# Moving the accumulator of a 31-tap depthwise convolution from SBUF to two PSUM banks

## What is computed

```python
h = rmsnorm(x, norm_mix_g)
z = h @ w_in                                   # 1024 -> 3*512 + 2*512
a_h, a_bg, a_cg, b_val, b_gate = split(z)      # 512 channels each
y_a = a_bg * dwconv(a_cg * a_h, conv_a_w)      # 3 taps
u = b_val * sigmoid(b_gate)
u = dwconv(u, conv_b_w) + conv_b_b             # 31 taps, 512 channels: the change
y_b = silu(layernorm(u, ln_b_g, ln_b_b))
x = x + concatenate([y_a, y_b]) @ w_out
```

## Time and profile before

| | |
|---|---|
| median of three runs | 2363.95 us |
| lowest and highest | 2361.16 and 2364.13 us |
| profiled execution, span from first to last instruction | 2362.2 us |
| PE busy | 2139.1 us (91% of the span) |
| DVE busy | 1606.9 us (68%) |
| POOL busy | 1067.2 us (45%) |
| ACT busy | 508.6 us (22%) |
| granted TensorE clock, mean | 0.963 of full |

### The profile page before, as it was taken

One profiled execution on the slowest core, in us unless ns is written; L12 is line 12 of the kernel. 1 busy time (PEld: TensorE's weight loads), 2 busy tenths in 40 slices (PEclk: granted clock), 3 DMA queues, 4 the chain that ended last, 5 costly groups with the idle time before them and its releaser, 6 DMA issues.

```text
span 2362.2 us, 24514 instructions
## 1 busy us (share of the span) xinstructions
PE 2139.1 (91%) x9224; PEld 1711.3 (72%) x9224; DVE 1606.9 (68%) x1645; ACT 508.6 (22%) x992; POOL 1067.2 (45%) x459
## 2 busy tenths in 40 slices
PE   3988868799999999999959999999999879879996
PEld 2876746588888888888737888788777558657885
DVE  8999987856666556667798455464483870795647
ACT  2211112321111111111232101001010331685112
POOL 6544553535544444456264353263262432342722
PEclk8998979999999999999979999999999989999998
DMA  4130111133123222333011111121021021000201
GB/s 145 38 97 27 36 36 36 36 134 101 61 87 107 97 94 93 107 107 107 27 45 41 40 46 53 36 62 44 29 69 36 18 71 30 16 28 1 72 18 72
DMA packets 42952, 141.71 MB, mean 60 GB/s; under 512 B 3568, under 2 KB 7808, under 8 KB 42880
## 3 DMA queue, kind: packets, MB, share of 16 engines
q1 hardware_dynamic: 29984, 101.38, 13.4%
q10 hardware_dynamic: 12896, 39.36, 4.7%
HBM read 136.50 MB, written 7.36 MB: 61 GB/s over the span
## 4 chain that ended last, share of the span: by engine, by line
PE 64%; DVE 31%; issue 2%; ACT 1%; POOL 1%; DMA 0%; DVEq 0%; SPq 0%; ACTq 0%; POOLq 0%
PE psum L439 20%; PE psum L441 20%; PE psum L440 20%; DVE glu L1264 10%; DVE temp L1494 3%; DVE temp L1152 2%; DVE norm_lo L1163 1%; DVE norm_lo L1161 1%; DVE top L1564 1%; DVE w_lo L1582 1%; DVE probs L1561 1%; DVE temp L1128 1%; PE psum L486 1%; PE psum L487 1%; PE psum L488 1%
## 5 line engine op out<-in xcount | busy, mean ns | idle before, releaser
L343 POOL TENSOR_TENSOR w_hi<-w_raw,zero 128x1024 fp32r<-128x1024 f32 x177 | 406.1, 2294 | 927.8 <-PE psum L441 838.8
L439 PE MATMUL psum<-norm_hi,w_hi 128*128 128x512 f32 x1712 | 672.6, 393 | 34.4 <-ACT temp L850 33.6
L441 PE MATMUL psum<-norm_hi,w_lo 128*128 128x512 f32 x1712 | 670.2, 391 | 0.0
L440 PE MATMUL psum<-norm_lo,w_hi 128*128 128x512 f32 x1712 | 670.0, 391 | 0.0
L346 POOL TENSOR_TENSOR w_lo<-w_raw,w_hi 128x1024 fp32r<-128x1024 f32 x177 | 501.4, 2833 | 13.9
L439 PEld LDWEIGHTS psum<-norm_hi,w_hi 128*128 128x128 f32 x1712 | 324.1, 189 | 106.0 <-issue 32.3
L441 PEld LDWEIGHTS psum<-norm_hi,w_lo 128*128 128x128 f32 x1712 | 323.6, 189 | 68.4
L440 PEld LDWEIGHTS psum<-norm_lo,w_hi 128*128 128x128 f32 x1712 | 324.2, 189 | 67.3
L1210 DVE SCALAR_TENSOR_TENSOR stream<-psum,mods,stream 128x512 f32<-128x512 f32 x160 | 118.5, 748 | 165.3 <-PE psum L441 165.2
L1264 DVE SCALAR_TENSOR_TENSOR glu<-glu,vec 128x1024 f32<-128x1024 f32 x120 | 226.0, 1884 | 4.1
L850 ACT ACTIVATE temp<-psum 128x512 f32<-128x512 f32 x160 | 91.8, 596 | 522.9 <-PE psum L441 441.8
(11 more groups left out here) (166 smaller groups left out, 3009.5 us busy)
## 6 DMA issues: line engine op xcount, KB each, us to landing
w_raw<-in_slabs SPq DMA_DIRECT2D x177, 512.0 KB, 3.5
ada_raw<-in_ada ACTq DMA_DIRECT2D x10, 3072.0 KB, 14.1
stream<-in_x SPq DMA_DIRECT2D x8, 512.0 KB, 8.6
out<-stream SPq DMA_DIRECT2D x8, 512.0 KB, 2.8
skew_scratch<-row_scratch ACTq DMA_DIRECT2D x1, 3072.0 KB, 15.0
ada_raw<-in_ada ACTq DMA_DIRECT2D x1, 2048.0 KB, 7.7
bias<-skew_scratch ACTq DMA_DIRECT2D x4, 512.0 KB, 3.7
c_act<-in_c ACTq DMA_DIRECT2D x1, 512.0 KB, 8.5
```

Source lines behind the costliest of these rows:

```text
L343: nc.gpsimd.tensor_tensor(WH[place][:, :], RAW[at % 2][:, :], zero[:, :].to_broadcast([P, 1024]), ALU.add).then_inc(w_hi_done, 1)
L439: nc.tensor.matmul(dst, wh, xh, start=n == 0, stop=False)
L440: nc.tensor.matmul(dst, wh, xl, start=False, stop=False)
L441: last = nc.tensor.matmul(dst, wl, xh, start=False, stop=n == len(terms) - 1)
```

## The change

The accumulator of each block becomes `ACC`, the PSUM banks 6 and 7 taken as one row of 1024 fp32 elements per partition. Tap 0 writes it, taps 1 to 29 read and write it in place, and tap 30 reads it and writes the result to the same SBUF buffer as before. The number, order, shape and waits of the instructions stay as they are.

```diff
         bank = [psum[:, n, :] for n in range(8)]
+        ACC = psum[:, 6:8, :].rearrange("p a b -> p (a b)")
...
                     j, tap = divmod(n, TAPS)
-                    u, c = UB[j], body(UB[(j + 4) % 5])
+                    u = UB[j]
                     w = v("conv_b", TAPS * j + tap)
                     window = u[:, 1 + tap:1 + tap + S]
                     if tap == 0:
                         dve.wait_ge(glu_done, 2 * j + 2)
                         if j:
                             dve.wait_ge(conv_done, j)
-                        step(nc.vector.tensor_scalar(c, window, w, v("conv_b_b", j), ALU.mult, ALU.add))
+                        step(nc.vector.tensor_scalar(ACC, window, w, v("conv_b_b", j), ALU.mult, ALU.add))
+                    elif tap < TAPS - 1:
+                        step(nc.vector.scalar_tensor_tensor(ACC, window, w, ACC, ALU.mult, ALU.add))
                     else:
-                        ins = nc.vector.scalar_tensor_tensor(c, window, w, c, ALU.mult, ALU.add)
-                        if tap == TAPS - 1:
-                            ins.then_inc(conv_done, 1)
-                        else:
-                            step(ins)
+                        nc.vector.scalar_tensor_tensor(body(UB[(j + 4) % 5]), window, w, ACC, ALU.mult, ALU.add
+                                                       ).then_inc(conv_done, 1)
```

## The result

The changed kernel takes 2302.94 us (median of four runs, 2299.07 to 2304.92) against 2363.89 for the kernel before: a ratio of 0.9741 with a 95% interval of 0.9727 to 0.9755. The forecast was 2305. The profiled execution has a span of 2300.7 us, 61.5 less. In the experiments they lie where their edits put them.

The account below looks back on a forecast made before the run. The prediction took DVE's taps, slowed beside POOL, to bound the stretch before the sums, with PE next. 58.3 us plus 1.5 for the clock less 1 gave span 2303.4, plus 1.75 for the median: 2305 us, range 2299 to 2333 (8 in 10).

Parts of the forecast that it names:

- what they share is used by a second SBUF input: DVE's taps beside POOL's splits: an accumulator in PSUM avoids the sharing that cost 71.8 us over 120 taps.
- The price of a tap: Undisturbed tap with its accumulator in PSUM: 1.285 us, 1.32 start to start; lower bound 1.07, upper 2.39.
- The 65 ns more: Documented PSUM access cost per tap, some 8 us for 124 taps; would move the forecast by at most 2 us.
- PE alone: PE's own work from 72.4 us, 195.8 for 36 tiles plus 5.6, brings it to the sums on line 536 at 273.8.
- the tail: DVE's last stretch before the sums, from 261 to 262: lines 1284 and 1286 2.6 to 6.1 us, six taps 7.9.
- Up to the sums I took 58.3: Start of the sums on line 536 moves from 332.8 to 274.5 us, and the rest of the kernel with it.
- for the clock 1.5: PE's sums: without the 19.6 us wait ahead of them, the granted clock of 0.81 over 8 us recovers 1.5 us.
- The 1 us that I took off: After the sums: 1 us deducted from the 59.8 us gain for slabs and products that meet otherwise.
- after each wait the granted clock is down for a time: PE before the sums: slow clock after waits explains some 11 of the 59.0 us between 273.8 and 332.8.
- Part of it is given back: Rival, chance 0.17: dearer taps, POOL's new timing or ACT keeping a bank; 2307 us at 1.40 per tap, 2332 at 1.6.
- Slower: Rival, chance 0.06: a bank serves only a read or a write at a time, tap 2.39 us, time 2430.
- No change: Rival, chance 0.03: POOL's use of SBUF as such slows the taps, so the time stays 2364 us.

Follow-up runs that it names:

- e1: Kernel before with the accumulator alternating: even taps write PSUM, odd taps and the last write SBUF; 2321.5 us, ratio 0.9812.
- e2: Kernel before, with GpSimd writing each low half of slabs 2 to 25 once more ahead of the real one; 2397.6 us (one run).
- e3: Changed kernel with GpSimd writing each low half of slabs 2 to 25 once more; 2307.4 us, ratio to the kernel before 0.9756.
- e9: Changed kernel with roots and pieces of the mixer, FFN and two attention norms in PSUM, and the pooling mixer norm's root; 2241.2 us, ratio 0.9484.
- e4: Changed kernel without taps 15 to 20 of each block (24 taps); 2303.6 us, ratio to the kernel before 0.9744.
- e7: Changed kernel with ten more taps ahead of the last six, reading ACC and writing banks 4 and 5; 2318.1 us (one run).
- e5: Kernel before without taps 15 to 20 of each block (24 taps); 2333.1 us (one run).

## Why the prediction was right

**The cause of the long taps: shown.** The step "what they share is used by a second SBUF input" stands on e1 (read against write in neighbouring taps), e2 and e3 (more of POOL's work costs one kind 28.6 us and the other nothing) and e9 (one line in two places, and two lines by turns beside the same slabs). The Trainium skill, SBUF — State Buffer, section Who interferes with whom, says that a VectorE instruction with two SBUF inputs contends with a GpSimd instruction that reads SBUF, and that one with at most one such input does not, unless it runs in one of the engine's 2-port modes, which a `tensor_scalar` can enter. The trace agrees with that in each of these runs.

**What the count of inputs leaves out.** Tap 0, a `tensor_scalar` with a single tensor input, was met by POOL as well in the kernel before:

```profile
L1262 DVE TENSOR_SCALAR glu<-glu,vec x4: 811/1212/2767, 74.5 to 266.4; 128x1024 f32<-128x1024 f32 x4
```

The one of 2767 ns starts at 74.45, beside POOL's line 346, the one of 811 at 144.4, with POOL idle. Which mode it ran in, no run tells. The prediction counted tap 0 as any other tap, and nothing in it hung on the difference: its four cost 6.0 us before and 5.4 after.

**The price of a tap: right, by 5 ns.** I took 1.285 us, and it is 1.290 with PSUM as source and destination, and 1.281 where tap 30 writes SBUF. That also decides what I could not bound well, the write and the bank read and written at once. The 65 ns more that the prediction worked out from the Trainium skill, VectorE: DVE Perf Modes, section on the TRN2 errata, do not show in the two-input taps: 5 are measured. Tap 0, which I counted as any other, takes 1.348 us.

**The bound behind the bound: right.** The step "PE alone" gave 273.8, and the sums start at 273.79. e4 shows that less of DVE's work ahead of the tail is worth nothing any more, e7 that more work in the tail costs its full length. PE and DVE's tail end within 0.06 us of each other, and no run made the tail shorter; that PE holds the sums by itself rests on its having no idle time ahead of them. For DVE I had an end between 271.5 and 276, and the last tap ends at 273.73: line 1286 took 3.30 and line 1284 1.55 us, 4.85 in the bounds of 2.6 to 6.1. POOL met line 1286 in two of the four blocks, for 2.0 us each, as much as I had allowed. The tail could start a little ahead of my 261 to 262 (260.91), since POOL's products no longer meet taps and take 1.32 us, where I had taken 1.8 to 2.3 from rows beside taps.

**The terms.** Up to the sums I took 58.3, and 59.0 is measured; for the clock 1.5, and 1.6 is measured. The 1 us that I took off for slabs and products that meet otherwise was not there; the later stages gave 0.9 more instead. Together these make the 2.7 us between the forecast span of 2303.4 and 2300.7 (0.7 + 0.1 + 1.0 + 0.9); in the medians 2.1 of them show. One sentence of the sum says too much: "after each wait the granted clock is down for a time". In the kernel before PE waits six times for ACT in this stretch. Behind the shortest two, 1.6 and 1.0 us, the clock stays at 1.00, and behind the other four, 3.7 to 11.5 us, it falls (0.50, the lower of its two levels, from 292 to 296 us, behind the wait of 4.2). All six waits are gone, so the forecast stands.

**The rivals.** "Part of it is given back" did not come about, since neither the write nor POOL's new timing cost PE anything. "Slower" needed a tap over 1.85 us. "No change" needed long taps to stay. One reading in the argument was too simple: I priced the loss as a property of the taps (71.8 us over 120 taps), and e5 showed that it is POOL's work that sets it. The forecast didn't depend on it, because the change takes the loss away as a whole; my expectation for e5 did.

## What to carry over

When one instruction of VectorE takes 1.3 us at one time and 2.8 or 3.3 at another, lay GpSimd's timeline beside it and count the tensor inputs in SBUF: with GpSimd at work, it pays to have one of the two in a free PSUM bank, and both engines gain. A line with one input, all in SBUF, can be met as well, as tap 0 was. Price such a loss by GpSimd's work in the stretch and not per instruction, and before you count the gain, add up what the next engine needs for the same stretch: here 71 us less on DVE could give no more than 59. Then look for other loops with two SBUF inputs on the path; here the norms' loops were worth as much as the convolution.

## What the hardware showed that I had not expected

A `tensor_scalar` of 128x1024 fp32 takes 1348 ns into PSUM; in the kernel before the same tap took 811 ns from SBUF to SBUF at its shortest, and 2767 at its longest. A single-input line loses its short time in PSUM, and it is dearer there than the two-input taps (1290). All four together still gain 0.6 us by the move, since none of them is lengthened beside POOL any more.
